# The S5 stage of a two-layer hybrid decoder step: sample tokens stepped for two channel tiles at a time beside the prompt's chain, and both rotated inputs formed on VectorE

## The reference: what is computed

```python
def s5_mixer(h, h0_re, h0_im, lam_re, lam_im, log_dt, b_re, b_im, c_re, c_im, d_skip, w_glu, b_glu):
    ab_re, ab_im, bb_re, bb_im = s5_discretize(lam_re, lam_im, log_dt, b_re, b_im)   # a = exp(lambda dt); B times a factor f
    bu_re = einsum("btgc,gpc->btgp", u, bb_re);  bu_im = einsum("btgc,gpc->btgp", u, bb_im)
    if h0_re is not None: ...                                  # samples: a * h0 is added at t = 0
    _, _, s_re, s_im = associative_scan(_s5_combine, ...)      # s[t] = a * s[t-1] + bu[t], complex
    y = einsum("btgp,gcp->btgc", s_re, c_re) - einsum("btgp,gcp->btgc", s_im, c_im)
    y = gelu(y.reshape(bsz, t, D_MODEL) + d_skip * hf)
    return y * sigmoid(y @ w_glu + b_glu), s_re[:, -1], s_im[:, -1]
```

## Time and profile before

| | |
|---|---|
| timed runs | 3963.7, 3961.18, 3957.25 us; median 3961.18 |
| profiled execution | 3958.59 us, span 3956.8 us |
| busy over the span | TensorE 59%, VectorE 73%, ScalarE 12%, GpSimd 39% |
| HBM read | 1399.77 MB, 355 GB/s over the span |
| S5 stage | first product of tile 0 at 45.2 us, first product of the next stage at 419.1 |
| the wait that costs the stage most | VectorE's scans for GpSimd's difference: 65.3 us in 14 waits |

### The profile page before, as it was taken

One profiled execution on the slowest core, in us unless ns is written; L12 is line 12 of the kernel. 1 busy time (PEld: TensorE's weight loads), 2 busy tenths in 40 slices (PEclk: granted clock), 3 DMA queues, 4 the chain that ended last, 5 costly groups with the idle time before them and its releaser, 6 DMA issues.

```text
span 3956.8 us, 32035 instructions
## 1 busy us (share of the span) xinstructions
PE 2319.9 (59%) x9698; PEld 1418.8 (36%) x9698; DVE 2874.7 (73%) x4146; ACT 459.3 (12%) x917; POOL 1541.0 (39%) x2027
## 2 busy tenths in 40 slices
PE   4666899100057787658599766562089873002777
PEld 2333668100022235658466336562056321000222
DVE  6777115999975567897767866777958867998555
ACT  6554021000000001220000001210000000000000
POOL 5999102543433333222323342223433443434332
PEclk8877999555589998879799988886599997556999
DMA  1001235799999999999999999999999999999998
GB/s 70 14 11 52 102 128 191 298 424 403 427 427 427 427 427 381 426 426 426 427 409 414 376 392 425 426 426 426 428 427 423 395 427 392 427 427 427 427 427 364
DMA packets 197416, 1404.63 MB, mean 355 GB/s; under 512 B 21952, under 2 KB 26304, under 8 KB 26768
## 3 DMA queue, kind: packets, MB, share of 16 engines
q0 software_dynamic: 167008, 1215.18, 73.3%
q1 hardware_dynamic: 30000, 187.74, 11.7%
q10 hardware_dynamic: 288, 0.18, 0.0%
HBM read 1399.77 MB, written 3.24 MB: 355 GB/s over the span
## 4 chain that ended last, share of the span: by engine, by line
DMA 50%; DVE 18%; PE 15%; POOL 8%; issue 7%; ACT 1%; POOLq 1%; DVEq 0%; ACTq 0%
DMA arena<-in_u_dram,ixs 27%; DMA arena<-in_v_dram,ixs 23%; DVE arena L1581 12%; PE ps L907 6%; PE ps L647 3%; POOL arena L437 3%; PE ps L687 2%; PE ps L805 2%; DVE ps L1601 1%; POOL arena L440 1%; POOL arena L444 1%; POOL arena L445 1%; POOL arena L503 1%; POOL arena L418 1%; POOL arena L441 1%
## 5 line engine op out<-in xcount | busy, mean ns | idle before, releaser
L907 PE MATMUL ps<-arena 128*128 128x512 f32 x2304 | 1122.7, 621 | 1187.7 <-DVE arena L1591 994.8
L1581 DVE CUSTOM_DVE_ANT_0 arena<-arena,ps 128x2048 f32<-128x2048 f32 x556 | 1255.9, 2284 | 194.6 <-DMA arena<-in_u_dram,ixs 180.8
L907 PEld LDWEIGHTS ps<-arena 128*128 128x128 f32 x2304 | 412.6, 194 | 1868.8 <-issue 1349.8
L1601 DVE SCALAR_TENSOR_TENSOR ps<-arena,ps 128x1024 f32<-128x1024 f32 x564 | 726.3, 1288 | 433.9 <-DMA arena<-in_v_dram,ixs 433.5
L503 POOL DMA_INDIRECT arena<-in_u_dram,ixs x560 | 546.8, 976 | 1035.8 <-DVE arena L1581 989.0
L503 POOL DMA_INDIRECT arena<-in_v_dram,ixs x576 | 554.9, 963 | 946.0 <-PE ps L907 799.2
L805 PE MATMUL ps<-HT,W 128*128 128x160 f32 (+1 forms) x3072 | 410.2, 296 | 76.8 <-ACT arena L1191 33.7
L805 PEld LDWEIGHTS ps<-HT,W 128*128 128x128 f32 x3072 | 405.1, 199 | 96.5 <-issue 80.1
L1591 DVE TENSOR_SCALAR arena<-ident,arena 128x128 f32<-128x128 f32 x576 | 164.8, 286 | 56.2 <-PE ps L907 52.2
L833 PE MATMUL ps<-W,arena 128*128 128x128 f32 x1024 | 124.1, 282 | 42.9 <-DVE arena L1706 16.5
L753 PE MATMUL ps<-HN,arena 128*32 128x256 f32 x512 | 139.5, 439 | 0.0
(11 more groups left out here) (250 smaller groups left out, 2159.3 us busy)
## 6 DMA issues: line engine op xcount, KB each, us to landing
W<-in_slabs_dram SPq DMA_DIRECT2D x168, 1024.0 KB, 10.1
arena<-in_u_dram,ixs POOLq DMA_INDIRECT x576, 16.5
arena<-in_v_dram,ixs POOLq DMA_INDIRECT x576, 16.7
GB<-in_norms_dram POOLq DMA_DIRECT2D x4, 1024.0 KB, 6.1
arena<-in_s_bc_dram SPq DMA_DIRECT2D x32, 128.0 KB, 2.1
X<-in_x_dram SPq DMA_DIRECT2D x3, 1024.0 KB, 10.6
out_y_dram<-HN SPq DMA_DIRECT2D x2, 1024.0 KB, 6.3
arena<-in_keys_dram POOLq DMA_DIRECT2D x1, 1024.0 KB, 5.0
```

The lines of the kernel that those rows point to most:

```text
L907: mm = nc.tensor.matmul(ps[:, 8 - SHARE + b, :], DG[(first + n) % DIAGS], ring[:, r, OWN + BANK * b:OWN + BANK * (b + 1)], start=(n == 0), ...
L1581: V.tensor_tensor_reduce(ring[:, r, :], ring[:, r, :], token, 1.0, 0.0, ALU.mult, ALU.add, AV[:, COL_AT[t] + n:COL_AT[t] + n + 1]).then_in ...
L1601: V.scalar_tensor_tensor(to, row, weight, total, ALU.mult, ALU.add).then_inc(row_used[r], 1)
```

## The change

1. GpSimd's difference M[2] - M[3] moves to VectorE, right behind the sum (semaphore `s5_wi` goes).
2. The samples of two tiles (pair j) are stepped together: instructions of 64 elements instead of 32, steps 0 and 1 beside the odd tile 2j+1, steps 2 and 3 beside the even tile 2j+2. Their states lie in HN instead of in the arena.
3. The samples' output products leave `s5_out_part` and become `s5_sample_part(j)`, which TensorE does behind the output part of tile 2j+2 (semaphores `s5_ys`, `s5_ysg`); `s5_out_part` does not wait for `s5_bsd`. Their gelu is one instruction a pair.
4. C, its negative and the diagonals have four slots instead of two; loads of B and C are written apart; all loops over tiles are written out.

```diff
@@ SyncE
+            def s5_b_tile(k):
+                if k >= 2:
+                    sp.wait_ge(s5_bx, k - 1)
+                sp.dma_start(BB[:, k % 2]..., s5_bc[k, :, 0:2 * P]).then_inc(s5_b_in[k % 2], 16)
+            def s5_c_tile(k):
+                if k >= 4:
+                    sp.wait_ge(s5_ys, (k - 4) // 2 + 1)
+                sp.dma_start(CB[:, k % 4]..., s5_bc[k, :, 2 * P:4 * P]).then_inc(s5_c_in[k % 4], 16)
...
@@ GpSimd
-            def sample_states(i, h):
-                pool.wait_ge(s5_bsc, k + 1)
-                a = [w[:, bass.ds(k * QK, QK)].unsqueeze(2).to_broadcast([P, QK, SB]) for w in (abr, abi)]
-                for step in range(ST):
+            def sample_steps(j, steps):
+                pool.wait_ge(s5_bsc, 2 * j + 2)
+                tiles = slice(2 * QK * j, 2 * QK * (j + 1))
+                a = [w[:, tiles].unsqueeze(2).to_broadcast([P, 2 * QK, SB]) for w in (abr, abi)]
+                for step in steps:
...
-                pool.wait_ge(s5_bur, 2 * i + h + 1)
-                nc.gpsimd.tensor_tensor(M[2], M[2], M[3], ALU.subtract).then_inc(s5_wi, 1)
-                sample_states(i, h)
-                        pool.wait_ge(s5_y, 2 * i + h)
-                    diagonal(*nxt)
+                if k % 2 == 1:
+                    sample_steps(k // 2, range(0, 2))
+                elif k >= 2:
+                    sample_steps(k // 2 - 1, range(2, ST))
+                if k + 1 < KT:
+                    diagonal(k + 1)
...
@@ TensorE
                 pe.wait_ge(s5_p, k + 1)
-                pe.wait_ge(s5_bsd, k + 1)
...
-                nc.tensor.matmul(ps[:, 7, 0:NS], DD[:, h, :], HT[:, bass.ds(k, 1), SEQ:NT]...)
...
+            def s5_sample_part(j):
+                pe.wait_ge(s5_bsd, j + 1)
+                if j > 0:
+                    pe.wait_ge(s5_ysg, j)
+                for e in range(2):
+                    k, out = 2 * j + e, slice(NS * e, NS * (e + 1))
+                    nc.tensor.matmul(ps[:, 7, out], DD[:, k % 4, :], HT[:, k, SEQ:NT], ...)
+                    for q in range(QK):
+                        for n, c in enumerate((CB[:, k % 4, 0, rows], CN[:, k % 4, rows])):
+                            mm = nc.tensor.matmul(ps[rows, 7, out], c, BSF[:, j % 2, n, at:at + NS], ...)
+                mm.then_inc(s5_ys, 1)
...
+            for k in range(KT):
+                if k + 1 < KT:
+                    s5_in_part(k + 1)
+                s5_out_part(k)
+                if k >= 2 and k % 2 == 0:
+                    s5_sample_part(k // 2 - 1)
...
@@ VectorE
-                settle(V.tensor_tensor(M[0], M[0], M[1], ALU.add))
+                V.tensor_tensor(M[0], M[0], M[1], ALU.add)
+                settle(V.tensor_tensor(M[2], M[2], M[3], ALU.subtract))
                 for src, dst in ((M[0], M[1]), (M[2], M[3])):
-                    if src is M[2]:
-                        dve.wait_ge(s5_wi, k + 1)
```

More of the change, by code:

```diff
@@ L420, in discrete_b @@
                 pool.wait_ge(pstep, st.next())
-                if not first:
+                if k > 0:
                     pool.wait_ge(s5_bt, k)
@@ L475, in _ @@
             pool.wait_ge(s5_pv, 3)
-            diagonal(0, 0)
-            discrete_b(0, 0, True)
-            per_tile = 1 + 3 * ST
-            s5_tile(0, 0, True)
-            s5_tile(0, 1)
-            with pool.Fori(1, KT // 2 - 1) as i:
-                st.enter(i - 1, 2 * per_tile)
-                s5_tile(i, 0)
-                s5_tile(i, 1)
-            st.leave(KT // 2 - 2)
-            s5_tile(KT // 2 - 1, 0)
-            s5_tile(KT // 2 - 1, 1, last=True)
+            diagonal(0)
+            discrete_b(0)
+            for k in range(KT):
+                s5_tile(k)
+            sample_steps(KT // 2 - 1, range(2, ST))
             pool.dma_start(s5s_out, SSO[:].rearrange("p c q b -> p (c q b)")).then_inc(stores, 16)
@@ L749, in s5_out_part @@
+                nc.tensor.matmul(ps[:, 5, 0:SEQ], DD[:, k % 4, :], HT[:, k, 0:SEQ], start=True, stop=False,
+                                 skip_group_check=True)
                 for q in range(QK):
                     rows = slice(QC * q, QC * (q + 1))
[L751 removed]
+                    cr, ci = CB[:, k % 4, 0, rows], CN[:, k % 4, rows]
                     for n, c in enumerate((cr, cr, ci, ci)):
[L753 removed]
@@ L754, in s5_out_part @@
-                    for n, c in enumerate((cr, ci)):
-                        mm = nc.tensor.matmul(ps[rows, 7, 0:NS], c, BSF[:, h, n, NS * q:NS * (q + 1)], start=False,
-                                              stop=(n == 1), skip_group_check=True)
+                        mm = nc.tensor.matmul(ps[rows, 5, 0:SEQ], c, PR[n][:, q, :], start=False, stop=(n == 3),
+                                              skip_group_check=True)
                 mm.then_inc(s5_y, 1)
-            s5_in_part(0, 0)
@@ L760, in _ @@
-            s5_in_part(0, 1)
-            s5_out_part(0, 0)
-            with pe.Fori(1, KT // 2) as i:
-                for h in range(2):
-                    s5_in_part(i, h)
-                    s5_out_part(2 * i + (h - 1), 1 - h)
-            s5_out_part(KT - 1, 1)
+            def s5_sample_part(j):
[4 more added lines that the diff above has]
+                    k, out = 2 * j + e, slice(NS * e, NS * (e + 1))
+                    nc.tensor.matmul(ps[:, 7, out], DD[:, k % 4, :], HT[:, k, SEQ:NT], start=True, stop=False,
+                                     skip_group_check=True)
+                    for q in range(QK):
+                        rows, at = slice(QC * q, QC * (q + 1)), NS * (QK * e + q)
+                        for n, c in enumerate((CB[:, k % 4, 0, rows], CN[:, k % 4, rows])):
+                            mm = nc.tensor.matmul(ps[rows, 7, out], c, BSF[:, j % 2, n, at:at + NS], start=False,
+                                                  stop=(n == 1), skip_group_check=True)
+                mm.then_inc(s5_ys, 1)
@@ L768, in _ @@
+            s5_in_part(0)
+            for k in range(KT):
+                if k + 1 < KT:
+                    s5_in_part(k + 1)
+                s5_out_part(k)
+                if k >= 2 and k % 2 == 0:
+                    s5_sample_part(k // 2 - 1)
+            s5_sample_part(KT // 2 - 1)
+            pe.wait_ge(s5_ysg, KT // 2)
             pe.wait_ge(s5_yg, KT)
@@ L1071, in _ @@
             turns(1)
-            s5_tile(0, 0, first=True, reuse=False)
-            s5_tile(0, 1, reuse=False)
-            with act.Fori(1, KT // 2 - 1) as i:
-                ast.enter(i - 1, 4)
-                s5_tile(i, 0)
-                s5_tile(i, 1)
-            ast.leave(KT // 2 - 2)
-            s5_tile(KT // 2 - 1, 0)
-            s5_tile(KT // 2 - 1, 1, last=True)
+            for k in range(KT):
+                s5_tile(k)
             gelu_y(KT - 1)
+            gelu_samples(KT // 2 - 1)
             with act.Fori(0, 4) as g:
@@ L1393, in fractions, with s5_tile @@
                 V.scalar_tensor_tensor(PRD, plus, ROUND, PRD, ALU.subtract, ALU.subtract).then_inc(s5_f, 1)
-            def s5_tile(i, h, first=False, last=False):
-                k = 2 * i + h
-                if not last:
+            def s5_tile(k):
+                if k + 1 < KT:
                     fractions(k + 1)
-                if not first:
+                if k > 0:
                     final_states(k - 1)
@@ L1439, in _ @@
             dve.wait_ge(norm_tp, 12)
-            s5_tile(0, 0, first=True)
-            s5_tile(0, 1)
-            with dve.Fori(1, KT // 2 - 1) as i:
-                st.enter(i - 1, 4)
-                s5_tile(i, 0)
-                s5_tile(i, 1)
-            st.leave(KT // 2 - 2)
-            s5_tile(KT // 2 - 1, 0)
-            s5_tile(KT // 2 - 1, 1, last=True)
+            for k in range(KT):
+                s5_tile(k)
             final_states(KT - 1)
             dve.drain().then_inc(s5_sf, 1)
-            dve.wait_ge(s5_y, KT)
+            dve.wait_ge(s5_ys, KT // 2)
             with dve.Fori(0, 4) as g:
```

186 lines of the change are left out of this document (89 added, 97 removed).

## The result

The changed kernel takes 3899.13 us (median of 4 runs, 3897.01 to 3901.38) against 3961.8 before: ratio 0.9844, 95% interval 0.9826 to 0.9861, 62.7 us faster. The forecast was 3895. Measured again it took 3896.89 (5 runs) against 3959.21: 0.9844 again (0.9831 to 0.9858).

What follows compares the result with a forecast made beforehand. GpSimd was taken to close the S5 stage's loop, both other engines waiting for it; 15 x (22.64 - 18.75) = 58.4, plus 1.1 and 4.1, is 63.6 us off 3958.59: 3895 us, range 3885 to 3915.

Steps and rivals of the forecast that it cites:

- (1): Subtraction moved from GpSimd to VectorE: plus 1.20 us a tile on VectorE, and the wait for GpSimd goes.
- (2): VectorE's own work per tile: sum 18.43 us, 18.75 with 0.3 allowed for scans beside 128-wide GpSimd instructions.
- (3): GpSimd's load: 35.5 of a pair's 37.5 us, nearly full but 5 us early where it is waited for.
- walk: GpSimd's schedule through a pair of tiles: Bs at T+23 and T+40.5, steps 2 and 3 ending at T+32.5.
- (4): TensorE from output products' start to input products' end: 15.5 us in one tile, 17.5 in the next with samples.
- (5): ScalarE's input for the fractions: ready 17.1 us after output products' start against 18.75, hidden by 1.7 us.
- rival A: TensorE and ScalarE close the loop: 20 us a tile with a longer low clock, 3915 us; chance 0.13.
- (7): Ends of the S5 stage: last tile gains 1.1 us; tail 12.0 instead of 16.1 us, a gain of 4.1.
- B: GpSimd's lock makes VectorE's two-operand instructions and scans wait: 21.4 us a tile, 3936 us; chance 0.05.
- D: Slower: TensorE stays at 1.2 GHz through the stage, 25.6 us a tile, 3998 us; chance 0.02.
- C: The gain is given back later, in the gathers' stages: up to half lost, 3927 us; chance 0.03.
- E: TensorE is not freed since the pair's states are late: 22 us a tile, 3945 us; chance 0.03.

Runs made afterwards that it cites:

- steps_none: Changed kernel with the sample tokens' steps left out on GpSimd; copies, diagonals and B stay: 3890.0 us, 18.55 us a tile.
- pool_more: Changed kernel with each sample step's four GpSimd multiplications made twice, 16 instructions of 64 elements a pair more: 3919.9 us.
- Grouped: Kernel before with the difference on VectorE and the samples' output products moved behind the prompt's sixteen: 3935.1 us.
- pairs_only: Changed kernel with the difference M[2] - M[3] put back on GpSimd: 3909.6 us, 19.67 us a tile.
- fewer: Changed kernel with real and imaginary part merged into one GpSimd instruction, same elements in 31 instructions a pair: 3907.4 us.

## Why the prediction was right

Forecast 3895, measured 3899 and 3897. The mechanism was the one forecast: GpSimd freed, VectorE without a wait, the gain carried whole to the end. Of the sum 58.4 + 1.1 + 4.1 = 63.6 the profile has 55.5 + 0.5 + 6.8 = 62.8; two terms were mis-sized, by -2.9 and +2.7 us, and nearly cancel. That the forecast is within 4 us is in part luck.

**The subtraction, (1) and (2).** 18.75 us a tile forecast, 18.94 measured. In the tile shown: up to the scans 7.13 (forecast 7.22), scans 5.37 (5.3 with the allowance), closing products to the next first product 6.50 (6.21). Over tiles 1 to 14 the three parts are 7.15, 5.41 and 6.46, 19.03 together; the first tile's 17.68 brings the mean to 18.94. The term that was too small is company, beside the scans (0.61 us over the 4.80 of the first tile, where the sum had about 0.46) and beside the closing products: I took 1.20 us from rows with 32-element instructions beside them, and now they have 64. Beside none they take 1.14, beside 32 elements 1.20, 64 about 1.27, 128 up to 1.39 (steps_none, 226.33 to 227.72), 256 up to 1.55.

**GpSimd, (3).** Instructions of 64 elements take 0.27 us free of company (four in 1.06); 0.30 was taken. The forecast wait of 3 us a pair is 2.7 (16.4 us in 6 waits). That GpSimd is nearly full was right, pool_more shows it. That its results stand 5 us early was not right. With T at 176.51, the start of the odd tile's fractions, the two Bs are ready at T+24.0 and T+42.1 (walk: T+23 and T+40.5), 3.0 and 4.2 us before TensorE transposes them at 203.42 and 222.81. The states with their copies are ready at 214.91, T+38.4 and not T+32.5: 0.15 us behind the closing products' end, where the walk had them 5 us ahead of it. The two copies, each beside a closing product, are 2.3 us of that:

```profile
212.62 2.29 POOL L458 COPY arena<-HN 128x64 f32<-128x64 f32 x2 [0.17 <-POOL HN L453]
```

It cost nothing, since TensorE asks for the states at 221.57.

**TensorE and ScalarE, (4) and (5).** 17.5 us forecast with samples, 12.8 measured; the turns end 12.3 us behind the start of the output part, not 17.1. The failing step is that nine small products save 0.65 us: I priced them by their own records, but their cost was in what they keep apart. Grouped, the output part is 2.5 us shorter at a like clock, and 18 samples at the end cost 1.24 us, under my lower bound of 1.3. The clock was the other part: I wrote that it should fall less and gave this no price. It was at its lower level for 3.0 us instead of 6.5, which at half speed is some 1.7 us. I estimate from these rows that of the 4.7 us between 17.5 and 12.8 the order is 2.2, the clock 1.7 and the samples 0.8. So margins were wide where I thought them thin, and rival A had nothing behind it: VectorE never waited. The Trainium skill's page TensorE: Matmul & The Clock Gate (Why this matters for your kernels) says that products of few output columns run side by side when each goes to its own group of 32 columns of the array. The trace agrees as far as it shows: four q groups, each on its own 32 output rows, overlap 2.4 times when nothing stands between them, and 1.6 times with the small products between.

**The ends, (7).** 9.3 us of tail instead of the 12.0 forecast, by the same shorter output part (7.0 us from 347.26 to 354.24). This is where the 2.7 us came back.

**Rivals.** B named a real mechanism with too high a price for 64-element instructions: 1.26 us a tile over VectorE alone, not 3.0. With longer instructions it comes true, in pairs_only by 2.1 us on the scans and in fewer by 0.7 us a tile. Both directions are in the traces: GpSimd gets on one for one beside closing products, and VectorE stands behind a long GpSimd instruction. Yet VectorE did not lose the whole length of a short one: 0.13 us for 0.27. The Trainium skill's page SBUF — State Buffer (Who interferes with whom), where the second to issue blocks until the first has ended, agrees with the first two; for short instructions on VectorE's side the measurement is milder. D did not occur: the granted clock is 0.81 and 0.82 over 100 to 300 us, still 0.50 at the start of output parts, and the engine has time for it. Its price was misread too: a mean of 0.65 from 213 to 215 puts the rise at 214.4 and not at 213.7, so 6.5 us ran at the lower level, and a tile at half clock all through would be 24.9 us, not 25.6. The forecast does not rest on that. C and E did not occur: the rest is 3538 to 3543 us, and TensorE never waited for the states.

## What to carry to other kernels

When the largest wait of a profile is taken away, ask which engine closes the loop: here the difference alone gave 21 us of 62, since the same engine was waited for at a second place. An engine at 99% busy may still hold time that is not work: compare its instruction pitch with the pitch of the same instructions in a stretch where GpSimd is idle. Give work beside such an engine to GpSimd in short instructions, place it where VectorE reads from PSUM (B beside those products cost nothing here), merge instructions on the engine that bounds, and keep small TensorE products from standing between large ones that go to different output rows.

## What the runs showed of the hardware that I had not expected

- Fewer and longer GpSimd instructions slow VectorE: 31 instead of 48 a pair, of the same elements, cost 0.72 us a tile, most of it in the scans, and possibly in part because they fall beside other VectorE instructions; VectorE's 1024-wide products from SBUF go from 1.14 us apart to 1.27 beside 64 elements and 1.55 beside 256.
- A stalled VectorE instruction counts as busy. In pairs_only VectorE is 99.5% busy and has no wait, while a scan of 0.74 us lasts 2.73.
- Two 32-column products behind every four of 256 columns stretch an output part from 8.0 to 10.4 us at a like clock, though each small one is recorded with 0.2 us.
